# SBUF byte positions of the operands of fp32r matmuls in a two-block transformer kernel

## What is computed

```python
def even_layer(x, ...):
    p = rmsnorm(x, g_norm) @ w_in            # q, k, v, o, z_a, gates, u, z_b
    ...
    return x + jnp.concatenate([y_a, y_b], axis=-1) @ w_out
def odd_layer(x, ...):
    p = rmsnorm(x, g_norm) @ w_in            # q, latent, index, z
    ...
    return x + (out * jax.nn.silu(z)) @ w_out
def swiglu(h, w_gu, w_down):
    gate, up = jnp.split(h @ w_gu, 2, axis=-1)
    return (jax.nn.silu(gate) * up) @ w_down
def second_block(x, ...):
    for layer in range(2):
        h = h + mixer(rms_norm(h, attn_norm[layer]))
        h = h + swiglu(rms_norm(h, ffn_norm[layer]), ffn_w_gu[layer], ffn_w_down[layer])
    return rms_norm(h, final_norm)
```

## Time and profile before

| | |
|---|---|
| median of 3 runs | 1989.58 us (1988.95 to 1989.74) |
| profiled execution, its span | 1987.9 us |
| TensorE matmuls busy | 1954.5 us, 98% of the span |
| VectorE, ScalarE, GpSimd busy | 1069.5, 773.0, 329.7 us |
| DMA | 187.15 MB, mean 94 GB/s |

### The profile page before, as it was taken

The page is one execution under the profiler, slowest core; times in us unless marked ns, Lnnn a source line. Parts: engine busy times, 40 slices in busy tenths (PEclk is TensorE's granted clock), DMA queues, the critical chain, the costliest instruction groups (busy, mean ns, idle before and its releaser), DMA issues.

```text
span 1987.9 us, 25351 instructions
## 1 busy us (share of the span) xinstructions
PE 1954.5 (98%) x9736; PEld 1513.6 (76%) x9736; DVE 1069.5 (54%) x2021; ACT 773.0 (39%) x1404; POOL 329.7 (17%) x417
## 2 busy tenths in 40 slices
PE   8999999999999999999999999999999999999998
PEld 6877777888777668757788888878766788888886
DVE  3567643444699765485544443343688554444332
ACT  3342433433354654474322222232566432222322
POOL 0550000001130751051000000030255300000000
PEclk9999999999999999999999999999999999999999
DMA  7552324442423123312333333365100133333322
GB/s 174 155 159 75 93 89 147 149 138 75 109 73 91 59 54 85 91 49 85 96 96 95 94 91 88 98 169 165 43 2 1 54 95 96 95 90 93 94 88 72
DMA packets 316782, 187.15 MB, mean 94 GB/s; under 512 B 33519, under 2 KB 297199, under 8 KB 316406
## 3 DMA queue, kind: packets, MB, share of 16 engines
q1 hardware_dynamic: 310254, 168.62, 30.1%
q10 hardware_dynamic: 6408, 16.91, 2.2%
HBM read 183.27 MB, written 17.96 MB: 101 GB/s over the span
## 4 chain that ended last, share of the span: by engine, by line
PE 91%; DVE 5%; ACT 2%; issue 1%; POOL 0%; ACTq 0%; DVEq 0%
PE banks L291 23%; PE banks L293 23%; PE banks L292 23%; PE banks L1957 3%; PE banks L1926 3%; PE banks L1940 2%; PE banks L399 2%; PE banks L401 2%; PE banks L400 2%; PE banks L878 1%; PE banks L886 1%; PE banks L979 1%; DVE prob L1994 1%; DVE win_prob L1994 0%; DVE wlo L2304 0%
## 5 line engine op out<-in xcount | busy, mean ns | idle before, releaser
L291 PE MATMUL banks<-xs,wlo 128*128 128x512 f32 x1336 | 538.8, 403 | 0.4 <-DVE wlo L2304 0.4
L293 PE MATMUL banks<-xs,whi 128*128 128x512 f32 x1336 | 528.3, 395 | 0.0
L292 PE MATMUL banks<-xs,whi 128*128 128x512 f32 x1336 | 528.2, 395 | 0.0
L2304 DVE TENSOR_TENSOR wlo<-raw,whi 128x1024 fp32r<-128x1024 f32 (+1 forms) x283 | 359.9, 1273 | 312.6 <-ACT whi L2295 312.1
L2295 ACT ACTIVATE whi<-raw 128x1024 fp32r<-128x1024 f32 (+1 forms) x283 | 293.6, 1039 | 231.4 <-PE banks L293 156.7
L291 PEld LDWEIGHTS banks<-xs,wlo 128*128 128x128 f32 x1336 | 251.0, 188 | 67.8 <-issue 7.5
L292 PEld LDWEIGHTS banks<-xs,whi 128*128 128x128 f32 x1336 | 251.1, 188 | 62.1 <-issue 3.4
L293 PEld LDWEIGHTS banks<-xs,whi 128*128 128x128 f32 x1336 | 251.0, 188 | 60.5
L505 POOL TENSOR_TENSOR squares<-squares,x_tmp 128x512 f32<-128x512 f32 x35 | 46.8, 1338 | 733.2 <-ACT x_tmp L497 733.2
L291 PE MATMUL banks<-a_hi,wlo 128*128 128x512 f32 x352 | 139.9, 397 | 0.0
L293 PE MATMUL banks<-a_hi,whi 128*128 128x512 f32 x352 | 139.4, 396 | 0.0
(11 more groups left out here) (395 smaller groups left out, 2904.9 us busy)
## 6 DMA issues: line engine op xcount, KB each, us to landing
raw<-in_ffn_w_gu SPq DMA_DIRECT2D x88, 512.0 KB, 3.8
raw<-in_e_w_in SPq DMA_DIRECT2D x56, 512.0 KB, 4.0
raw<-in_ffn_w_down SPq DMA_DIRECT2D x32, 512.0 KB, 4.0
s_skew<-s_bias ACTq DMA_DIRECT2D x6, 2560.0 KB
raw<-in_o_w_in SPq DMA_DIRECT2D x21, 512.0 KB, 4.1
raw<-in_e_w_out SPq DMA_DIRECT2D x16, 512.0 KB, 4.1
raw<-in_b_w_in SPq DMA_DIRECT2D x15, 512.0 KB, 4.0
raw<-in_ffn_w_down SPq DMA_DIRECT2D x16, 384.0 KB, 3.4
```

The lines of the kernel that those rows point to most:

```text
L291: nc.tensor.matmul(out, k.wlo[:, chunk.slot, at, :], self.x_hi(kt), start=first, stop=False)
L292: nc.tensor.matmul(out, k.whi[:, chunk.slot, at, :], self.x_lo(kt), start=False, stop=False)
L293: ins = nc.tensor.matmul(out, k.whi[:, chunk.slot, at, :], self.x_hi(kt), start=False, stop=last)
L2304: self.nc.vector.tensor_tensor(self.wlo[:, chunk.slot, 0:chunk.blocks, :], self.raw[:, chunk.slot, 0:chunk.blocks, :], hi.bitcast(F32), AL ...
```

## The change

A function `line_up` moves the next free byte forward to byte 128 of a row of 512. It is called ahead of `raw`, of the areas of the first layer, of `oT`, of the tiles of each attention and of the feed-forward's tiles. `xs` is put 256 bytes behind a lined-up byte, at 384. The tiles of the first feed-forward get 528 columns of which 512 are used, so that each begins 64 bytes further in its row than the one before. Nothing else is changed: the instructions, their order, their shapes and their waits are the same.

| operand | byte before | byte after |
|---|---|---|
| `whi`, `wlo` | 128 | 128 |
| `xs_hi`, `xs_lo` | 352 | 384 |
| `yb_e`, `yb_g`, `ya_c` | 128 | 128 |
| `yb_j` | 160 | 128 |
| `ya_a` | 0 | 128 |
| `ckv_hi`, `ckv_lo` | 256 | 128 |
| `odd_hi`, `odd_lo` (for `o_out`) | 352, 32 | 128, 128 |
| `win_hi`, `win_lo` (for `a_out`) | 160, 32 | 128, 128 |
| `long_hi`, `long_lo` (for `b_out`) | 64, 32 | 128, 128 |
| `a_hi0`, `a_lo0`, tile k | 32, 32 | 128 + 64 k, 64 k |
| `a_hi1`, `a_lo1` | 96, 96 | 128, 128 |

```diff
--- before.py
+++ after.py
@@ -51,6 +51,7 @@
 AHEAD = 2
 TILE_BANKS = 3
 SUM_BANK = 3
+ROW, ROW_AT = 512, 128
 
 
 class Signal:
@@ -2154,6 +2155,11 @@
         self.stage_n += 1
         return self.nc.alloc_sbuf_tensor_at(f"{name}_{self.stage_n}", shape, dt, offset=at)
 
+    def line_up(self):
+
+        self.room_used = (self.room_used + ROW - 1 - ROW_AT) // ROW * ROW + ROW_AT
+        return self.room_used
+
     def sb(self, ctx, name, shape, dt=F32):
 
         at = self.room_used
@@ -2345,11 +2351,13 @@
         self.hT = tensor("hT", [P, MT, 512])
         self.ident = tensor("ident", [P, P])
         self.ones = tensor("ones", [P, P])
+        self.line_up()
         self.raw = tensor("raw", [P, SLOTS, 8, P])
         self.whi = tensor("whi", [P, SLOTS, 8, P], F32R)
         self.wlo = tensor("wlo", [P, SLOTS, 8, P], F32R)
         self.gains = tensor("gains", [P, 7, MT])
-        self.xs_at = self.room_used
+        self.xs_at = self.line_up() + ROW // 2
+        self.room_used = self.xs_at
         self.xs = tensor("xs", [P, 2, MT, 512], F32R)
         self.xs_hi, self.xs_lo = self.xs[:, 0], self.xs[:, 1]
         self.xtmp = tensor("x_tmp", [P, 2, 512])
@@ -2383,22 +2391,22 @@
             head_sq = self.sb(c, "head_sq", [P, QT, 4])
             row_scale = self.sb(c, "column_scale", [P, QT])
             tri = self.sb(c, "tri", [P, P])
-            a_at = self.room_used
+            a_at = self.line_up()
             v = self.sb(c, "v_rows", [P, QT, 4, 257])
             b_at = self.room_used
             h = self.sb(c, "heads", [P, QT, 4, 257])
-            c_at = self.room_used
+            c_at = self.line_up()
             u = self.sb(c, "u", [P, MT, 512])
             wp = self.sb(c, "wp", [P, 4, 2, 256])
-            e_at = self.room_used
+            e_at = self.line_up()
             win = self.sb(c, "win", [P, 2, 2, 512])
             cnt = self.sb(c, "cnt", [P, 4, 512])
-            g_at = self.room_used
+            g_at = self.line_up()
             qk = self.sb(c, "qk", [P, MT, 512])
             h_at = self.room_used
             pad = self.sb(c, "pad", [P, 2, 516])
             decay = self.sb(c, "decay", [P, 2, 1280])
-            j_at = self.room_used
+            j_at = self.line_up()
             everywhere = self.sb(c, "gate_rows_all", [P, 4, 512])
             xin = self.place("xin", [P, QT, DM], F32, a_at)
             gi = self.place("gates", [4, 2, 512], F32, b_at)
@@ -2630,7 +2638,7 @@
         xh, xl = (lambda k: hi[:, k, :]), (lambda k: lo[:, k, :])
         rb = self.rb[:, :]
         with ExitStack() as c2:
-            q_at = self.room_used
+            q_at = self.line_up()
             qT = self.sb(c2, "qT", [P, MT, 512])
             kT = self.sb(c2, "kT", [P, MT, 512])
             vt = self.sb(c2, "vt2", [P, QT, DM])
@@ -2651,7 +2659,7 @@
                 members = self.place("members", [P, MT, P], F32R, self.o_at + 6 * 2048)
                 oR = self.place("squares_rounded", [P, 2, 512], F32R, self.o_at + 4 * 2048)
                 stat = self.sb(c3, "odd_stat", [P, 4, 3, 2])
-                latent_at = self.room_used
+                latent_at = self.line_up()
                 spread_in = qT[0:112, 0:2, :].rearrange("p a (b c) -> p (a b) c", b=4)
                 ch = self.sb(c3, "ckv_hi", [P, 2, 512], F32R)
                 cl = self.sb(c3, "ckv_lo", [P, 2, 512], F32R)
@@ -2820,7 +2829,9 @@
         hi, lo = self.xs_hi, self.xs_lo
         rb = self.rb[:, :]
         T = DFF // P
-        a_hi, a_lo = self.sb(c, f"a_hi{layer}", [P, T, 512], F32R), self.sb(c, f"a_lo{layer}", [P, T, 512], F32R)
+        self.line_up()
+        skew = 16 if layer == 0 else 0
+        a_hi, a_lo = [self.sb(c, f"{name}{layer}", [P, T, 512 + skew], F32R)[:, :, 0:512] for name in ("a_hi", "a_lo")]
         tmp = self.ff_tmp
 
         def steps(n):
@@ -2858,7 +2869,7 @@
             vb = self.sb(c2, "value_blocks", [P, 2, P])
             seen = self.sb(c2, "seen", [P, 1])
             with ExitStack() as c3:
-                w1_at = self.room_used
+                w1_at = self.line_up()
                 w1 = self.sb(c3, "cmp_w1", [P, 2, 16, 256])
                 bias_all = self.place("bias_all", [P, NH, 512], F32, w1_at)
                 c_at = self.room_used
@@ -2943,7 +2954,7 @@
         k.setup()
         stages = k.even()
         with ExitStack() as c:
-            k.o_at = k.room_used
+            k.o_at = k.line_up()
             k.oT = k.sb(c, "oT", [P, MT, 512])
             k.win_small = k.sb(c, "win_small", [P, 44])
             stages += k.odd() + k.windowed()
```

## The result

The changed kernel takes 1956.51 us (median of 4 runs, 1955.66 to 1957.14) against 1989.66 us before: a ratio of 0.9834, 95% interval 0.9823 to 0.9846, 33.2 us less. The forecast was 1950.0 (1945 to 1982). The profiled execution spans 1954.2 us, 33.7 less than before.

The account below looks back on a forecast made before the run. TensorE, 98% busy, was taken to bound the kernel, mostly 6,696 products times their spacing. Savings per operand summed to 39.7 us, taking the median from 1989.58 to 1950 us, range 1945 to 1982.

Parts of the forecast that it names:

- That the spacing depends on the byte, and 384 is like 128: fp32r products: 226.7 ns where moving and stationary bytes agree, 232.5 to 235.0 where they differ; 384 inferred at 226.7; chance 0.68.
- two pairs 256 apart: Moving bytes 352 and 96 (both 233.3 ns), 0 and 256 (232.5 and 232.7): taken to show a repeat every 256 bytes.
- A repeat of 512: Rival: `xs` at 384 stays slow, only tiles brought to 128 gain, 9.2 us, 1980 us; chance 0.20.
- half a row as the worst byte: Rival: the 4584 products at a difference of 256 get slower, 2002 us at 238 ns each; chance 0.07.
- no effect of the address: Rival: spacing follows something else, such as PSUM bank or stage order; the change does nothing, 1989.6 us; chance 0.05.
- the term of `xs` and of the row-wise products: Products moving `xs` or holding it stationary, 352 to 384: 6.67 ns saved each, 26.7 us and 3.8 us.
- a wait that appeared there would have to be 0.16 us per tile: Feed-forward tiles: weights' splits stay ahead of PE as tiles shrink from 5.60 to 5.44 us; only such a wait takes the gain.
- The first down projection: First feed-forward's 528 products with 64-byte steps: 234.2 to 230 ns, 2.2 us saved, between +4.0 and -0.4.
- The second one: Second feed-forward's down projection, both tiles from byte 96 to 128: 528 products save 6.67 ns each, 3.5 us.
- Nothing for the fp32 operands: fp32 operands that move too (`qT`, `kT`, `prob`, `vt` and so on): no change, as no stage showed a dependence to price.
- the bound of 4 us: If some 2000 fp32 transposes and value products felt 2.1 ns each, the time would move 4 us either way.

Follow-up runs that it names:

- `xs_128`: The changed kernel with the normed input `xs` at byte 128 instead of 384: 1956.48 us, ratio 0.9837 to before.
- the scans: Three runs of the changed kernel whose gate-and-up stages read moving or stationary operands s bytes further on: 1968.70, 1963.76 and 1966.15 us, only spacings read.

## Why the prediction was right

**That the spacing depends on the byte, and 384 is like 128.** Right, and shown directly: the gate-and-up tile is at 5.44 us, `xs_128` and the changed kernel differ by 0.03 us, and the scans have the period of 256. The inference was from two pairs 256 apart with like values, which was thin, as the prediction said, so that it held was in part luck; the scans show that values of `s` 256 apart are alike.

**Rivals.** A repeat of 512, half a row as the worst byte, and no effect of the address are out by the same tile. The Trainium skill, TensorE: Matmul & The Clock Gate (Step-by-step: what each phase is for), has loading the next weights take nothing from the running matmul, because the read ports are two. In these runs moving the stationary operand alone by 32 bytes, with the same work, costs 6.3 ns per product (226.8 to 233.1), so for fp32r a product's time does depend on where the weights lie relative to what moves. The N / 2.4 + 2.5 ns (215.7 for 512 columns) of the Trainium skill, TensorE: Matmul & The Clock Gate (Wait — 56ns, not 53.3ns?), was reached in no stretch: the shortest mean over 12 fp32r products in any trace here is 226.6 ns.

**The step that was mis-sized** is the term of `xs` and of the row-wise products, "4008 x 6.67 ns = 26.7 us" and "576 x 6.67 = 3.8 us". Both took every product as part of an undisturbed sequence on an engine that nothing else holds back. Measured alone they give 25.2 us instead of 30.5. The 2112 products of the gate-and-up stages gave 14.0 of 14.1. The others gave some 11 of 16.4: about 1.8 us in products that settle after a disturbance, 1.8 us in the one stretch where VectorE is nearly full (1.9 predicted with the latent products, 0.1 measured), and the remaining 1.5 to 2 us in waits that grew by some tenths each, as in the row-wise products of `e_v`, which saved 0.6 of 1.3 us with a wait for `wlo` among them, and in products that are followed by another kind of matmul and so were no 6.67 ns to begin with. This last part is read from the traces, not tested. The median has another half a microsecond less than the profiled execution (33.2 and 33.7 us), which fits the clock's drop in two of four executions. The sentence that the cover holds ("a wait that appeared there would have to be 0.16 us per tile") was checked for the feed-forward alone, where it was true; VectorE's share of the other stages was not looked at.

**The first down projection** was put at 230 ns and measured 231.1, 1.6 us saved instead of 2.2. The sign of the steps was not asked: against like tiles at 128 they cost 2.4 us. The second one saved 3.2 instead of 3.5, as its tiles have other matmuls between them, behind which the products settle.

**Nothing for the fp32 operands.** The third attention took 141.0 us before and 141.0 after, the other two 70.6 and 70.7, 55.3 and 55.3 (from the last product ahead to the first behind), so the bound of 4 us wasn't needed.

## What to carry to other kernels

In a stream of fp32r matmuls of 512 columns, compare the start-to-start spacing in the timeline between tiles of different addresses; a single stage whose operands change their byte within a tile shows the dependence without any run. Put all moving and stationary operands of a stream at the same byte modulo 256, and on a multiple of 32; it costs some hundred bytes per tile group and gave 3% of each product. Before a gain per instruction is multiplied by a count, take out of the count the products just behind another kind of matmul and the stages where another engine is nearly full too (VectorE here with 79.3 of 85.8 us). And compare runs of two variants only after a look at the granted clock of each stretch: here it made 1.6 of the 2.7 us of one experiment.

## What was unexpected of the hardware

The spacing isn't a constant but a short cycle: at byte 352 the starts in the timeline alternate between 235 and 231 or 232 ns apart, and at the like position all are 226 or 227. Behind another kind of matmul it takes some products to get there (231.7 ns over the first six, above). Moving all operands together by 4 bytes costs 10 ns per product (237.8), more than any multiple of 32 does. A faster stream of products brought the granted clock down in a stretch where before it was full: the waits in it grew, and the products behind them took 425 ns.
